# The feed-forward opening of a decoder step on one core: sums of squares added up on VectorE, operand work moved to GpSimd

## What is computed

```
x = x + rmsnorm(ox @ x_wo, nrm[3])        # end of cross-attention
h = rmsnorm(x, nrm[4])
u = causal_dwconv(h @ f_wu)               # width 3, D_FF = 2816
x = x + rmsnorm((gelu(u) * (h @ f_wg)) @ f_wd, nrm[5])
```

## Time and profile before

| what | us |
|---|---|
| median of 3 runs | 2245.98 (2242.68 to 2252.88) |
| profiled execution, its own time | 2251.43 |
| span of the profiled execution | 2249.4 |
| TensorE busy | 2160.9 |
| VectorE busy | 1285.9 |
| ScalarE busy | 841.4 |
| GpSimd busy | 619.2 |
| mean granted clock of TensorE | 0.971 |

### The profile page before, as it was taken

One profiled execution on the slowest core, in us unless ns is written; L12 is line 12 of the kernel. 1 busy time (PEld: TensorE's weight loads), 2 busy tenths in 40 slices (PEclk: granted clock), 3 DMA queues, 4 the chain that ended last, 5 costly groups with the idle time before them and its releaser, 6 DMA issues. The chain is left out here.

```text
span 2249.4 us, 42839 instructions
## 1 busy us (share of the span) xinstructions
PE 2160.9 (96%) x17101; PEld 1972.5 (88%) x17101; DVE 1285.9 (57%) x2350; ACT 841.4 (37%) x1720; POOL 619.2 (28%) x519
## 2 busy tenths in 40 slices
PE   9999998989999989999999999998899999999997
PEld 6799977866656689999999988998899999999997
DVE  5213354357776741232255254577898978866957
ACT  5222253126656730111343133554433334334453
POOL 5000035422323022111112200332344443345643
PEclk9999999879999999999999999998999999999998
DMA  4321097983545131110401354332232332264234
GB/s 145 107 61 44 29 204 243 311 284 124 167 135 171 71 120 43 61 57 29 162 29 38 121 198 188 99 114 86 91 124 91 105 110 72 106 238 170 93 125 146
DMA packets 133714, 276.35 MB, mean 123 GB/s; under 512 B 24626, under 2 KB 79571, under 8 KB 128332
## 3 DMA queue, kind: packets, MB, share of 16 engines
q1 hardware_dynamic: 110796, 232.32, 31.0%
q0 software_dynamic: 10368, 28.33, 3.9%
q10 hardware_dynamic: 12352, 12.96, 1.8%
HBM read 229.49 MB, written 48.26 MB: 123 GB/s over the span
## 5 line engine op out<-in xcount | busy, mean ns | idle before, releaser
L88 PE MATMUL psum<-merged_high,oq_half 128*128 128x352 f32 x768 | 189.0, 326 | 1.8 <-POOL oq_half L69 1.4
L88 PE MATMUL psum<-ff_t,ff_x_slots 128*128 128x264 f32 x1200 | 149.1, 284 | 1.3 <-DVE ff_x_slots L69 1.3
L88 PEld LDWEIGHTS psum<-ff_t,ff_x_slots 128*128 128x128 f32 x1200 | 147.1, 188 | 1.6 <-issue 1.5
L88 PEld LDWEIGHTS psum<-merged_high,oq_half 128*128 128x128 f32 x768 | 135.2, 190 | 2.5 <-POOL oq_half L69 1.9
L2006 ACT ACTIVATE na_pt<-psum 128x512 f32<-128x512 f32 (+1 forms) x170 | 86.8, 545 | 106.3 <-PE psum L1881 89.9
L88 PE MATMUL psum<-x_half_high,mg_w_high 128*128 128x352 f32 x384 | 124.0, 323 | 2.0 <-ACT gated L2390 1.2
L88 PE MATMUL psum<-h_again_low,mg_w_high 128*128 128x352 f32 x384 | 123.1, 321 | 0.0
L88 PE MATMUL psum<-x_half_high,mg_w_low 128*128 128x352 f32 x384 | 123.0, 320 | 0.0
L88 PE MATMUL psum<-ff_bslot,ff_x_slots 128*128 128x264 f32 x888 | 117.3, 285 | 0.7 <-DVE ff_z L4355 0.7
L69 POOL TENSOR_TENSOR ff_x_slots<-low,ff_x_slots 128x512 fp32r<-128x512 f32 x52 | 82.2, 1595 | 113.1 <-ACT ff_x_slots L3803 109.0
L88 PEld LDWEIGHTS psum<-ff_bslot,ff_x_slots 128*128 128x128 f32 x888 | 112.0, 189 | 1.0 <-DVE ff_z L4355 0.9
(11 more groups left out here) (668 smaller groups left out, 5604.7 us busy)
## 6 DMA issues: line engine op xcount, KB each, us to landing
na_kv<-in_pool POOLq DMA_DIRECT2D x128, 128.0 KB, 4.0
na_kv<-in_pool SPq DMA_DIRECT2D x128, 128.0 KB, 3.6
ff_bslot_raw<-mid_ops SPq DMA_DIRECT2D x59, 264.0 KB, 3.1
mid_ops<-ff_bufs SPq DMA_DIRECT2D x11, 1056.0 KB, 3.9
mg_w<-in_w_merge SPq DMA_DIRECT2D x15, 768.0 KB, 4.4
ring<-in_f_wu SPq DMA_DIRECT2D x11, 1024.0 KB, 5.4
low<-in_f_wg SPq DMA_DIRECT2D x22, 512.0 KB, 4.3
first_pages<-in_pool SPq DMA_DIRECT2D x68, 128.0 KB, 5.5
```

The lines of the kernel that those rows point to most:

```text
L88: ins = nc.tensor.matmul(out, w[a], x[b], start=first and n == 0, stop=last and n == 2)
```

## The change

Groups 2 and 3 get the tree that groups 0 and 1 have, so TensorE's `sums2` is three matmuls for every group. In VectorE's order `tree(2)` stands where `sums_early(0)` stood, in front of `scale(3)`; `sums_early(0)` moves behind the factor of the third group, and `tree(3)` stands behind it, both in front of `normed(2)`. The second half of t3's sum and the low parts of both halves of t3 and of t1 move from VectorE to GpSimd, where they stand in a row behind the weight low of product 10. What is computed stays the same, but for the order in which squares are added.

```diff
-        T_POOL, T_DVE = (("t3", 0),), (("t1", 0), ("t1", 1), ("t2", 0), ("t2", 1), ("t3", 1), ("t4", 0), ("t4", 1))
+        T_POOL, T_DVE = (("t3", 0), ("t3", 1)), (("t1", 0), ("t1", 1), ("t2", 0), ("t2", 1), ("t4", 0), ("t4", 1))
-        LOW_POOL = [("b22", 0)]
-        LOW_DVE = [("b11", 0), ("b21", 0), ("b11", 1), ("b21", 1), ("b22", 1), ("t2", 0), ("t2", 1), ("t3", 0), ("t3", 1), ("t1", 0), ("t1", 1),
-                   ("t4", 0), ("t4", 1)]
+        LOW_POOL = [("b22", 0), ("t3", 0), ("t3", 1), ("t1", 0), ("t1", 1)]
+        LOW_DVE = [("b11", 0), ("b21", 0), ("b11", 1), ("b21", 1), ("b22", 1), ("t2", 0), ("t2", 1), ("t4", 0), ("t4", 1)]
@@ TensorE, sums2
-                if g < 2:
-                    pe.wait_ge(S["tree"], 3 * (g + 1))
-                    column_sums(SUM2, y[:, 0, 0, col(g)], NT * g, "sum2_ready")
-                    return
-                pe.wait_ge(S["sq2_ready"], 2 * (g + 1))
+                pe.wait_ge(S["tree"], 3 * (g + 1))
                 if g == 2:
                     pe.wait_ge(S["h_ready"], 16)
-                else:
+                elif g == 3:
                     pe.wait_ge(S["scaled"], 8)
-                for t in range(NT):
-                    for k in range(KD):
-                        a = HG * (g - 2) + TW * t
-                        last = nc.tensor.matmul(psum[0:TW, second(g), NT * g + t:NT * g + t + 1], y[:, 1, k, a:a + TW], K["ones"][:, 0:1],
-                                                start=k == 0, stop=k == KD - 1)
-                last.then_inc(S["sum2_ready"], 1)
+                column_sums(second(g), y[:, g // 2, 0, col(g % 2)], NT * g, "sum2_ready")
@@ GpSimd
             low_of(10)
+            operand_low("t3", 0)
+            t_sum("t3", 1)
+            operand_low("t3", 1)
+            operand_low("t1", 0)
+            operand_low("t1", 1)
@@ VectorE
-            sums_early(0)
+            tree(2)
             scale(3)
             add(3, 0)
             add(3, 1)
             mean(SUM2, 1, third, "sum2_ready", 3, "mean2_ready")
             factor(1, third, "root2_ready", 2, "rstd2_ready")
+            sums_early(0)
+            tree(3)
             normed(2, range(KD))
@@
-            t_sum("t3", 1)
             weight_low(0, 7)
-            operand_low("t3", 0)
             evac(2, "c11")
-            operand_low("t3", 1)
-            operand_low("t1", 0)
             evac(0, "u2")
-            operand_low("t1", 1)
```

## The result

The changed kernel takes 2254.14 us (median of 22 runs, 2248.0 to 2257.53); the kernel before took 2246.91 us in as many. The ratio is 1.0021, with a 95% interval of 1.0012 to 1.0029: 4.7 us slower, 2.7 to 6.5. That is within the 0.5% called no change ahead, and its sign is that of the forecast (+4.5 us, 2250.5).

What follows compares the result with a forecast made beforehand. From about 1544 us to 1640 VectorE's queue was taken as the bound, a relay before it. 2.7 us gained at M1, then 29.0 instead of 21.8, put M2 4.5 later: 2246 + 4.5 = 2250.5, range 2237.5 to 2258.

Steps and rivals of the forecast that it cites:

- Steps 1 and 2: Relay up to spread2(2): fewer sum matmuls save TensorE about 8 us; scale(3) starts 0.5 later; TensorE idles 3.4.
- M1: The end of normed(3), 1546.96 us before the change; forecast 1544.25, 2.7 us earlier.
- its bound: In front of normed(3): if GpSimd holds the factor's reciprocal as well, M1 gains 2.0 us.
- Step 5: From M1 to M2: VectorE and GpSimd exclude each other, lengths add to 29.0 us instead of 21.8; TensorE idles 8.
- M2: The end of t4's low parts, 1568.79 us before the change; forecast 1573.25, 4.5 later.
- 12.0 + 2.2: GpSimd's work behind M1: five moved operations, 12.0 us, and unfinished weight lows of products 9 and 10, 2.2 us.
- Bounds: Limits: without exclusion VectorE needs 16.1 us behind M1 and product 12 comes 9 earlier; upwards +8 us.
- Step 6: Behind M2 nothing changes: product 11 comes 4.5 us later, and TensorE has no gap from 1640 us to catch up.
- No collision: Rival behind M1: no collision worth the name, VectorE's shorter queue wins; -9 us, 2237; chance 0.18.
- VectorE first always: Rival behind M1: VectorE's back-to-back queue keeps GpSimd out until about 1556; 2252; chance 0.62, shared with the serial case.
- The clock: Rival: the 8 us gap puts products 7 to 10 whole into the slow clock, 3 us each; +12, 2258; chance 0.06.

Runs made afterwards that it cites:

- relay_only: Changed kernel with t3's second sum and the four low parts put back on VectorE, trees and order kept; ratio to the kernel before 0.9992.
- move_only: Kernel before with only t3's second sum and the four low parts moved to GpSimd, no new trees; ratio to the kernel before 1.0019.
- writes_twice: Changed kernel with each of GpSimd's five moved instructions replaced by two fills with zeros, so its products differ; ratio to the kernel before 0.9969.
- s4_early: relay_only with the weight sum s4 of step 0 moved from in front of normed(3) to in front of normed(2); ratio to the kernel before 0.9986.
- tree3_lows: Changed kernel without group 2's tree, the five moved operations back on VectorE, weight lows of products 9 and 10 there too; ratio to before 0.9987.

## Why the prediction was right, point by point

- **Steps 1 and 2** (trees, relay). `scale(3)` at M0 + 3.37 and the factor's end at M0 + 9.82 (9.85 worked out). TensorE's stop in front of `spread2(2)` was 3.58 us (3.4). Right. That the first tree is no gain was implied and is now shown: without it `scale(3)` starts 0.5 us earlier and the 48 matmuls cost 0.3 (1.0 in the slow clock).
- **Steps 3 and 4** (M1). The hold of s4 is there, 2.63 us. M1 came 3.1 us earlier counted from M0 (2.7). The factor isn't held, so its bound falls. TensorE's half product ran in the fast clock (1.71 us, at 1535.30), which changed nothing, as said: in relay_only it took 2.99 us, and M1 is the same (23.69).
- **Step 5** (M1 to M2). 28.25 us instead of 29.0. TensorE's stop was 8.12 us (8). What is mis-sized is GpSimd's term, 12.0 + 2.2: of seven instructions of GpSimd behind M1 six held VectorE, for 11.0 us in all (1.0, 1.1, 2.2, 2.2, 2.3 and 2.2: each row's length less its free length), and one ran while VectorE read PSUM at 1562.98 and 1564.82 and waited 1.15 us for product 7. I had added all lengths, 14.2 us, 3.2 too much. Two terms were left out of the sum, the other way: VectorE's two reads of PSUM, 1.25 us, which stand in the 16.1 us of "Bounds" and not in the 29.0, and that wait of 1.15 us. So 16.1 + 11.0 + 1.15 = 28.25, and that 29.0 is off by 0.8 only is partly luck. M2 is +3.3 us from M0 (4.5); move_only shows the same 0.8 short.
- **Step 6** (nothing behind M2). P12 + 3.3, the rest 671.2 us in both.
- **The rivals.** "No collision" is refuted by the changed kernel, relay_only and move_only, and writes_twice shows about what it would have been: M2 7.6 us earlier than in the changed kernel, M2 and product 12 4.3 us earlier than before, and not 9. "VectorE first always" didn't happen here, but happened once in another order, where it cost 7 us; I had taken its price as 1 us more than turns, since in this kernel VectorE would have had to wait for product 7 early. "The clock": the stop of 8.12 us was followed by nearly 6 us at 0.50, so the slow clock did come, but not for products 7 to 10 whole, and it didn't move M2 past what VectorE's queue gives; VectorE's 1.15 us of waiting for product 7 falls beside a GpSimd instruction. What M2 would be with product 7 in the fast clock no run shows.
- **The total.** 4.5 forecast, 3.3 by the marks, 3.7 by the spans, 2.7 to 6.5 by the runs. That 4.5 lies so near the 4.7 of the ratio is luck within about 1 us, since the marks give 3.3. The forecast of 2250.5 was made on a median of three runs, 0.9 us under that of 22; the measured median is 3.6 above it.

What stays open: what decides whether a waiting GpSimd gets its turn. Two executions of one kernel differ, with GpSimd asking 0.06 us behind VectorE in both.

Of the versions that compute the same, only s4_early is faster than the kernel before by its whole interval (0.9975 to 0.9996). One of eleven, and so close to 1, can be chance. By its marks tree3_lows is the earliest in front of product 12 (3.2 us), apart from the order in which the lock-out was seen.

## What to carry to other kernels

Before work is taken from VectorE to GpSimd, ask what VectorE does at that time: if it makes operations with two SBUF inputs back to back, a GpSimd instruction that reads SBUF adds its length to VectorE's queue, and an operation that takes 1.18 us on VectorE and 2.4 on GpSimd is a loss. In these traces it is free only beside reads of PSUM and waits; here `normed` gave 3.3 us of such cover, and it was taken already. Taking work off TensorE gains only where another engine waits for it: of two equal trees that of group 3 shortened the relay, that of group 2 took 0.3 us of waiting away and made `scale(3)` 0.5 us later. And a microsecond gained in front of such a queue can be lost in it: relay_only kept 1.1 of 3.1 us.

## What the runs showed of the hardware that was not expected

- GpSimd can be shut out: 12.87 us for 1.3 us of work, while VectorE had eleven operations with two SBUF inputs queued without a gap; in a second execution of the same program it got its turn after one. No other instruction of GpSimd in this stage of the traces is lengthened by more than 1.1 us, about one operation of VectorE.
- GpSimd fills that only write SBUF (0.98 us for 1056 columns) hold nobody: 1.24 us for VectorE's operation beside them.
- A reciprocal with one SBUF input, 88 x 3, passes beside a GpSimd instruction in 0.17 us.
- A held instruction looks busy in the profile: VectorE's busy time rose from 1285.9 to 1296.6 us, although the five operations that left it (5.9 us) weigh more than the six of the trees that came (4.9 us).
